# Branch splits between the head norms, another bank pair for the first late gate, and an out projection with a loop of its own

## The reference: two layers of a hybrid decoder trunk

```python
h = h + 0.5 * swiglu(rmsnorm(h, norm_ffn1), ...)              # D_FF = 2816
x = rmsnorm(h, norm_mix)
z = x @ w_in + b_in                                           # mixers' inputs and 4 x 1024 gate columns
# four branches, 256 wide each
br_conv = silu(layernorm(conv + conv_b, conv_ln_g, conv_ln_b))
br_ret  = silu(r_g) * head_norm(r_o, ret_gn, center=True)
br_gla  = silu(g_r) * head_norm(g_o, gla_gn, center=False)
br_diff = head_norm(d_o, diff_subln, center=False) * (1.0 - lam_init)
gate   = sigmoid(gates.reshape(B, L, 4, 1024))
merged = einsum('blnc,ncd,blnd->bld', branches, w_branch, gate)
h = h + merged @ w_out
h = h + 0.5 * swiglu(rmsnorm(h, norm_ffn2), ...)
```

## Time and profile before

| | |
|---|---|
| median of 3 runs | 3060.79 us (3059.02 to 3063.26) |
| the profiled execution | 3066.44 us, of which the span of the core is 3064.9 |
| TensorE's mean granted clock | 0.975 of full speed |
| busy: PE, VectorE, ScalarE, GpSimd | 95%, 68%, 42%, 4% of the span |
| HBM | 104 GB/s over the span |

### The profile page before, as it was taken

One profiled execution on the slowest core, in us unless ns is written; L12 is line 12 of the kernel. 1 busy time (PEld: TensorE's weight loads), 2 busy tenths in 40 slices (PEclk: granted clock), 3 DMA queues, 4 the chain that ended last, 5 costly groups with the idle time before them and its releaser, 6 DMA issues.

```text
span 3064.9 us, 60838 instructions
## 1 busy us (share of the span) xinstructions
PE 2908.1 (95%) x21640; PEld 2779.2 (91%) x21640; DVE 2088.7 (68%) x3658; ACT 1285.0 (42%) x2206; POOL 120.8 (4%) x219
## 2 busy tenths in 40 slices
PE   4999999999899999999989999999989999999998
PEld 3999999887778989999989999998877889999998
DVE  7999534567556669996489993346664566799955
ACT  5555323335215245554255552233441242555533
POOL 0000001220000000000000000112100000000000
PEclk9999999999889999999999999999998999999999
DMA  3222225552213312223212222437422243122222
GB/s 112 96 87 98 97 82 176 164 191 81 82 59 142 136 59 88 85 93 110 83 57 96 95 98 96 139 117 202 143 79 80 74 148 119 56 96 94 97 97 88
DMA packets 102125, 320.89 MB, mean 105 GB/s; under 512 B 13503, under 2 KB 30063, under 8 KB 100272
## 3 DMA queue, kind: packets, MB, share of 16 engines
q1 hardware_dynamic: 89424, 277.03, 26.2%
q0 software_dynamic: 12512, 41.43, 4.3%
HBM read 290.62 MB, written 29.12 MB: 104 GB/s over the span
## 4 chain that ended last, share of the span: by engine, by line
PE 82%; DVE 6%; issue 6%; ACT 3%; POOLq 1%; DMA 1%; POOL 1%; DVEq 0%; ACTq 0%
PE ps L1226 41%; PE ps L1255 32%; PE ps L1386 3%; PE ps L1640 1%; PE ps L1238 1%; PE ps L1502 1%; POOLq L562 1%; DVE w_lo L1746 1%; DMA rets_out<-ss 0%; ACT hT L1013 0%; PE ps L1518 0%; POOL vpage L563 0%; PE ps L1480 0%; ACT w_hi L714 0%; DVE x_more L1832 0%
## 5 line engine op out<-in xcount | busy, mean ns | idle before, releaser
L1746 DVE TENSOR_TENSOR w_lo<-w_raw,w_hi 128x1024 fp32r<-128x1024 f32 x240 | 292.8, 1223 | 399.5 <-ACT w_hi L674 394.2
L1255 PE MATMUL ps<-x_more,w_hi 128*128 128x296 f32 x2112 | 462.1, 300 | 14.6 <-DVE p_copy L1902 12.6
L674 ACT ACTIVATE w_hi<-w_raw 128x1024 fp32r<-128x1024 f32 x224 | 235.5, 1054 | 528.4 <-PE ps L1226 198.2
L1255 PE MATMUL ps<-x_hi,w_hi 128*128 128x296 f32 x1408 | 426.3, 303 | 25.1 <-ACT p_copy L778 11.8
L1255 PE MATMUL ps<-x_hi,w_lo 128*128 128x296 f32 x1408 | 425.6, 302 | 0.0
L1255 PE MATMUL ps<-x_lo,w_hi 128*128 128x296 f32 x1408 | 425.3, 302 | 0.0
L714 ACT ACTIVATE w_hi<-w_raw 128x512 fp32r<-128x512 f32 x445 | 272.3, 629 | 306.8 <-PE ps L1255 192.7
L1226 PE MATMUL ps<-x_hi,w_hi 128*128 128x296 f32 x1600 | 377.7, 318 | 14.7 <-ACT hT L1013 9.3
L1255 PEld LDWEIGHTS ps<-x_more,w_hi 128*128 128x128 f32 x2112 | 353.7, 190 | 16.0 <-issue 13.6
L1226 PE MATMUL ps<-x_hi,w_lo 128*128 128x296 f32 x1600 | 356.5, 305 | 0.0
L1226 PE MATMUL ps<-x_lo,w_hi 128*128 128x296 f32 x1600 | 356.2, 305 | 0.0
(11 more groups left out here) (350 smaller groups left out, 4986.9 us busy)
## 6 DMA issues: line engine op xcount, KB each, us to landing
w_raw<-wstream SPq DMA_DIRECT2D x420, 512.0 KB, 3.5
kpage<-cache_k SPq DMA_DIRECT2D x128, 128.0 KB, 3.0
vpage<-cache_v POOLq DMA_DIRECT2D x128, 128.0 KB, 3.3
gate_rows<-hT SPq DMA_DIRECT2D x48, 296.0 KB, 2.1
d_sg<-gate_rows SPq DMA_DIRECT2D x16, 888.0 KB, 4.6
h_rows<-hT SPq DMA_DIRECT2D x2, 1480.0 KB, 6.1
hT<-h_rows SPq DMA_DIRECT2D x2, 1480.0 KB, 10.6
hT<-h_in SPq DMA_DIRECT2D x4, 592.0 KB, 8.3
```

What stands on the lines that cost most here:

```text
L674: act.activation(w_hi[:, slot, :, :], w_raw[:, slot, :, :], ACT.Copy).then_inc(weights_high, 1)
L1255: mm = pe.matmul(ps[:, bank, 0:HALF], wp[:, k, :], xp, start=new and k == 0 and n == 0, stop=k == KH - 1 and n == 2, skip_group_check=True)
L1746: v.tensor_tensor(w_lo[:, slot, :, :], w_raw[:, slot, :, :], w_hi[:, slot, :, :].bitcast(F32), ALU.subtract).then_inc(weights_low, 1)
```

## The change

1. *Head norms and branches on VectorE.* After norms 0 to 3 VectorE multiplies tiles 4 and 5 by their SiLU gates, waits for the mixers' stores, makes `br_hi` of the first four tiles of `FINISHED` itself (`tensor_copy`) and then their `br_lo`. Norms 4 to 6, the convolution's bias and tiles 2 and 3 follow. The low parts of weights 22 and 23, which stood between these steps, stand at the end of `branches`.
2. *ScalarE.* `br_hi` is made for the last four tiles only. Gates 22 and 23 are taken out of PSUM without their weight splits; the tanh of the convolution stands ahead of gate 23; the splits of weights 22 and 23 stand behind the tanh of late gate 0.
3. *The late gate of m = 0* is in pair 2, and PE doesn't wait for the tanh of gate 23 before it. Before branch 2 of m = 0 (also pair 2) PE waits for that late gate's tanh.
4. *The order in a merge step.* `m_hi` and `m_lo` are made before the second weight split of the step, no longer after it. The loops over m of PE and ScalarE are unrolled.
5. *Out projection.* PE has a function of its own for it, unrolled. It opens when branch 1 of m = 7 is taken (pair 1 empty) and seven tiles are ready. There is no drain, and the wait for all four branches stands behind unit 0.
6. *SP.* The first two `load_gates` are issued right after the weight load of f = 21, no longer after all stores of gate rows.

```diff
@@ -443,6 +443,11 @@
+def late_pair(m):
+return 3 if m else 2
 FINISHED = (6, 7, 4, 5, 2, 3, 0, 1)
@@ -530,12 +535,13 @@
         load_at(U_GATES + 2 * RING + f)
+        if f == 21:
+            sp.wait_ge(gla_s_state, 1)
+            load_gates(0)
+            load_gates(1)
     for s in range(STAGES):
         sp.wait_ge(gates_stored[s], 16 * KD * EARLY // STAGES)
     sp.wait_ge(h_spilled, 16)
-    sp.wait_ge(gla_s_state, 1)
-    load_gates(0)
-    load_gates(1)
     sp.dma_start(hT[:, 0:SPILLED, :], h_rows).then_inc(h_back, 16)
@@ -1141,37 +1147,39 @@
         square(4 + i, branch_tiles[tile])
-    gate_out(l, 22)
+    gate_activated(l, 22)
     for i in range(4, 7):
         act.wait_ge(hn_normed, i - 3)
         root(i)
     for i in range(4, 7):
         inverse(i)
-    gate_out(l, 23)
-def branches():
+def branches(l):
+    act.wait_ge(hn_normed, 7)
+    act.wait_ge(conv_done, 2)
+    for i in range(2):
+        act.activation(hn_root[:, i, :], Z[:, CG + i, :], ACT.Tanh, scale=0.5).then_inc(act_tanh, 1)
+    gate_activated(l, 23)
     act.wait_ge(mixers_stored, 16 * MIXER_STORES)
     for n, b in enumerate(FINISHED):
-        if n == 4:
-            act.wait_ge(conv_done, 2)
-            for i in range(2):
-                act.activation(hn_root[:, i, :], Z[:, CG + i, :], ACT.Tanh, scale=0.5).then_inc(act_tanh, 1)
-        act.wait_ge(hn_normed, 7)
-        act.wait_ge(br_ready, n + 1)
-        act.activation(br_hi[:, b, :], branch_tiles[b], ACT.Copy).then_inc(br_high, 1)
+        if n >= 4:
+            act.wait_ge(br_ready, n + 1)
+            act.activation(br_hi[:, b, :], branch_tiles[b], ACT.Copy).then_inc(br_high, 1)
 def gates(l):
-    with act.Fori(0, 2) as i:
-        for mm in range(4):
-            m = i * 4 + mm
-            quad, slot = l * QUADS + U_MERGE // RING + i * 2 + mm // 2, mm % 2 * 2
-            unit_done(quad, slot)
-            act.activation(split_cols(d_late[:, :]), pair(3), ACT.Tanh, scale=0.5, bias=hb[:, ds(m + 8 * EARLY, 1)]).then_inc(gate_tanh, 1)
-            split_high(quad + 1, slot)
-            act.wait_ge(merged_steps, m * 3 + 3)
-            split_high(quad + 1, slot + 1)
-            act.activation(m_hi[:, ds(m, 1), :], d_acc[:, 0:1, :], ACT.Copy, scale=0.5).then_inc(merged_high, 1)
+    for m in range(KD):
+        quad, slot = l * QUADS + U_MERGE // RING + m // 2, m % 2 * 2
+        unit_done(quad, slot)
+        act.activation(split_cols(d_late[:, :]), pair(late_pair(m)), ACT.Tanh, scale=0.5,
+                       bias=hb[:, m + 8 * EARLY:m + 8 * EARLY + 1]).then_inc(gate_tanh, 1)
+        if m == 0:
+            for f in (22, 23):
+                split_high(l * QUADS + (U_GATES + f) // RING + 1, f % RING)
+        split_high(quad + 1, slot)
+        act.wait_ge(merged_steps, m * 3 + 3)
+        act.activation(m_hi[:, m, :], d_acc[:, 0, :], ACT.Copy, scale=0.5).then_inc(merged_high, 1)
+        split_high(quad + 1, slot + 1)
     act.drain().then_inc(mixers_left, 1)
@@ -1205,7 +1213,7 @@
     head_norms(l)
-    branches()
+    branches(l)
     gates(l)
...
@@ -1328,18 +1336,12 @@
...
@@ -1698,22 +1700,38 @@
     pe.sem_inc(phases_entered, 1)
-    with pe.Fori(0, 2) as i:
-        for mm in range(4):
-            m = i * 4 + mm
-            quad, slot = l * QUADS + U_MERGE // RING + i * 2 + mm // 2, mm % 2 * 2
-            unit_ready(quad, slot)
+    for m in range(KD):
+        quad, slot = l * QUADS + U_MERGE // RING + m // 2, m % 2 * 2
+        unit_ready(quad, slot)
+        if m:
             pe.wait_ge(gate_tanh, m + KD * EARLY)
-            products(3, slot, (0, 8), 0, x_hi, x_lo).then_inc(units_multiplied, 1)
-            unit_ready(quad, slot + 1)
-            pe.wait_ge(br_split, 8)
-            for b in range(4):
-                if b in (0, 3):
-                    pe.wait_ge(branch_taken, m * 4 + 4 + b // 3)
-                last = products(BRANCH_BANKS[b], slot + 1, (2 * b, 2 * b + 2), 2 * b, br_hi, br_lo)
-                last.then_inc(*((branch_products, 1) if b < 3 else (units_multiplied, 1)))
-    pe.wait_ge(branch_taken, 4 * KD + 4)
-    pe.drain().then_inc(mixers_left, 1)
+        products(late_pair(m), slot, (0, 8), 0, x_hi, x_lo).then_inc(units_multiplied, 1)
+        unit_ready(quad, slot + 1)
+        pe.wait_ge(br_split, 8)
+        for b in range(4):
+            if b in (0, 3):
+                pe.wait_ge(branch_taken, m * 4 + 4 + b // 3)
+            if m == 0 and b == 2:
+                pe.wait_ge(gate_tanh, KD * EARLY + 1)
+            last = products(BRANCH_BANKS[b], slot + 1, (2 * b, 2 * b + 2), 2 * b, br_hi, br_lo)
+            last.then_inc(*((branch_products, 1) if b < 3 else (units_multiplied, 1)))
+def out_projection(l):
+    for m in range(KD):
+        pe.wait_ge(residual_added, l * 24 + 8 + m + 1)
+        unit_ready(l * QUADS + (U_OUT + m) // RING, m % RING)
+        bank = OUT_PAIRS[m % 4]
+        if m == 0:
+            pe.wait_ge(branch_taken, 4 * KD + 2)
+            pe.wait_ge(merged_ready, l * KD + KD - 1)
+            products(bank, 0, (0, KD - 1), 0, m_hi, m_lo, stop=False)
+            pe.wait_ge(merged_ready, l * KD + KD)
+            products(bank, 0, (KD - 1, KD), KD - 1, m_hi, m_lo, start=False).then_inc(units_multiplied, 1)
+            pe.wait_ge(branch_taken, 4 * KD + 4)
+            pe.sem_inc(mixers_left, 1)
+        else:
+            products(bank, m % RING, (0, KD), 0, m_hi, m_lo).then_inc(units_multiplied, 1)
@@ -1733,7 +1751,7 @@
     gates(l)
-    residual(l, 8, U_OUT, (8,), m_hi, m_lo)
+    out_projection(l)
     ffn(l, 1, U_FFN2)
@@ -2405,38 +2423,49 @@
-    for i in range(7):
-        if i == 4:
-            gate_low(l, 22)
+    def finished(b, c):
+        v.scalar_tensor_tensor(branch_tiles[b], Z[:, c, :], 0.5, branch_tiles[b], ALU.mult, ALU.mult).then_inc(br_ready, 1)
+    for i in range(4):
+        normed(i)
+    v.sem_inc(br_ready, 2)
+    v.wait_ge(hn_normed, 4)
+    finished(4, GR)
+    finished(5, GR + 1)
+    v.wait_ge(mixers_stored, 16 * MIXER_STORES)
+    for n in range(4):
+        b = FINISHED[n]
+        v.wait_ge(br_ready, n + 1)
+        v.tensor_copy(br_hi[:, b, :], branch_tiles[b]).then_inc(br_high, 1)
+    for n in range(4):
+        branch_low(n)
+    for i in range(4, 7):
         normed(i)
     v.wait_ge(hn_normed, 7)
     for j in range(2):
         ins = v.tensor_scalar(Z[:, CG + j, :], Z[:, CG + j, :], prm[:, P_LB + j:P_LB + j + 1], None, ALU.add)
     ins.then_inc(conv_done, 1)
-    v.sem_inc(br_ready, 2)
-    for b, c in ((4, GR), (5, GR + 1), (2, RG), (3, RG + 1)):
-        v.scalar_tensor_tensor(branch_tiles[b], Z[:, c, :], 0.5, branch_tiles[b], ALU.mult, ALU.mult).then_inc(br_ready, 1)
+    finished(2, RG)
+    finished(3, RG + 1)
+def branch_low(n):
+    b = FINISHED[n]
+    v.wait_ge(br_high, n + 1)
+    v.tensor_tensor(br_lo[:, b, :], branch_tiles[b], br_hi[:, b, :].bitcast(F32), ALU.subtract).then_inc(br_split, 1)
 def branches(l):
-    def low(n):
-        b = FINISHED[n]
-        v.wait_ge(br_high, n + 1)
-        v.tensor_tensor(br_lo[:, b, :], branch_tiles[b], br_hi[:, b, :].bitcast(F32), ALU.subtract).then_inc(br_split, 1)
-    v.wait_ge(br_ready, 6)
-    for n in range(4):
-        low(n)
-    gate_low(l, 23)
     for n in range(2):
         v.wait_ge(act_tanh, 5 + n)
         link(v.tensor_scalar(hn_root[:, n, :], hn_root[:, n, :], 1.0, 0.5, ALU.add, ALU.mult))
         v.tensor_tensor(branch_tiles[n], branch_tiles[n], hn_root[:, n, :], ALU.mult).then_inc(br_ready, 1)
     v.wait_ge(br_ready, 8)
     for n in range(4, 8):
-        low(n)
+        branch_low(n)
+    gate_low(l, 22)
+    gate_low(l, 23)
 def gates(l):
-    v.wait_ge(mixers_stored, 16 * MIXER_STORES)
     clear_sum(3 * l + 3)
@@ -2458,11 +2487,11 @@
                     v.tensor_tensor(d_acc[:, 0, :], d_acc[:, 0, :], d_acc[:, 1, :], ALU.add).then_inc(merged_steps, 1)
-            split_low(quad + 1, slot + 1)
             v.wait_ge(merged_steps, m * 3 + 3)
             v.wait_ge(merged_high, m + 1)
             v.scalar_tensor_tensor(m_lo[:, ds(m, 1), :], d_acc[:, 0:1, :], 0.5, m_hi[:, ds(m, 1), :].bitcast(F32),
                                    ALU.mult, ALU.subtract).then_inc(merged_ready, 1)
+            split_low(quad + 1, slot + 1)
             v.wait_ge(merged_ready, l * KD + m + 1)
```

More of the change, by code:

```diff
@@ L1320, in ffn, with residual @@
                 pe.sem_inc(units_multiplied, 2 * KF)
-            def residual(l, r0, first, blocks, xh, xl, hidden=None):
+            def residual(l, r0, first, blocks, xh, xl, hidden):
                 units = len(blocks)
@@ L1330, in residual @@
                             bank = OUT_PAIRS[j]
-                            if hidden is not None and j == 0:
+                            if j == 0:
                                 for k in range(blocks[u]):
@@ L1336, in residual @@
                                 last.then_inc(units_multiplied, 1)
-                            elif hidden is None and j == 0:
```

(4 more changed lines are left out.)

## The result

Five runs of either kernel gave 3044.38 us (3040.80 to 3045.83) after and 3060.06 us (3057.14 to 3063.26) before: a ratio of **0.9946, 95% interval 0.9931 to 0.9960**, 12 to 21 us less. Ratios in this document are the ones on record; they aren't the quotients of the two medians beside them, from which they differ by up to 0.0017. The forecast was 3043.0 us. The profiled execution of the changed kernel took 3044.62 us, its span 3043.1.

What follows compares the result with a forecast made beforehand. PE, busy 95% of 3064.9 us, bounds the kernel through waits and slow clock. Gains 6.1 + 5.6 + 7.6 = 19.3 us, one dip leaves 17.8: 3048.6 profiled, median 5.65 lower, 3043.0 us; 8 in 10 for 3037 to 3051.

Steps and rivals of the forecast that it cites:

- The late gate: Opening of the merge, m = 0: starts at 966.50 instead of 967.50, without the 0.84 us wait for gate 23's tanh.
- VectorE's queue: Opening of the merge: copies and subtractions hidden before norm 4; first branch product at 973.8, after 0.6 us of PE idling.
- The new stall: Before branch 3 of m = 0, PE waits 1.8 us in each layer until VectorE has taken branch 0.
- The queues: SP's loads: earlier gate loads and later weight loads cost nothing; weights issued 13 us before need, landing in 3.5 us.
- The out projection: After m = 7: 3.8 us a layer, 2.2 wait and restart plus 1.6 clock; 7.6 us in both layers.
- The sum: Both layers' merges: 6.1 + 5.6 + 7.6 = 19.3 us gained, if the new stall costs only its length.
- The dip: PE's clock falling behind the new stall, 1.5 us each; one taken for two layers, leaving a gain of 17.8 us.
- The time: Whole kernel: profiled execution 3048.6 us, median 5.65 us below it, so 3043.0 us, 0.58% less.
- (b): Rival: PE's slow clock lasts after the new stall in both layers, 5 to 6 us each; 3050 to 3052 us; chance 0.10.
- (c): Rival: half delivers; branch chain not shortened, or out projection finds another wait; 3050 to 3054 us; chance 0.10.
- (d): Rival: stall only moves; branch 3's wait grows and out projection waits for m_lo; 3058 to 3061 us; chance 0.05.
- (e): Rival: slower, SP's queue holds a load and weights of m = 3 arrive late; 3067 us or more; chance 0.03.

Runs made afterwards that it cites:

- e2_bank_only: Kernel before with PE's and ScalarE's loops over m unrolled and the late gate of m = 0 on pair 2, without its wait for gate 23; ratio 1.0011.
- e9_same_bank: Changed kernel with the late gate of m = 0 back on bank pair 3, behind gate 23's tanh; 3056.46 us, ratio 0.9963.
- e5_late_gate_loads: Changed kernel with SP's first two gate loads back behind all stores of gate rows; 3056.73 us, ratio 0.9986.
- the two experiments: Kernel before with the new out projection and earlier m_hi and m_lo, ratio 0.9985; changed kernel with the old out projection, ratio 0.9954.
- e4_old_out: Changed kernel with the old out projection (wait for four branches, drain), the new order of m_hi and m_lo kept; 3050.71 us, ratio 0.9954.
- e10_scalar_and_first: Changed kernel with VectorE's memset before weight split 22, branch 0 right behind it, and the first four br_hi on ScalarE; 3046.94 us, ratio 0.9943.
- e8_longer_stall: Changed kernel with two more waited memsets on VectorE at m = 0, ahead of the existing one; one execution, 3050.92 us.
- e6_scalar_splits: Changed kernel with the first four high parts of the branches made by ScalarE, no copies on VectorE; 3043.96 us, ratio 0.9933.

## Why the prediction was right, step by step

- **The late gate.** Right: no wait there, and it starts 1.0 us earlier, as put. `e2_bank_only` shows that this is worth nothing while the last `br_lo` comes late. The 8 us of `e9_same_bank` are another thing, which the sum didn't price: with the old pair PE waits 2.49 us for gate 23's tanh, which the change itself lets end 1.6 us later than before, and loses clock behind it.
- **VectorE's queue.** The copy took 0.46 us, its lower bound. The first branch product was put at 973.8 on the scale of before, 35.97 us after the first square; it came at 35.87. VectorE's first taking was put at 979.6, 41.77 after; it came at 41.74. The low parts ended 7.1 us after the start of the late gate, inside the 7.3 that the prediction gave as its limit.
- **The new stall.** It is there, in both layers, where it was put. Forecast 1.8 us, measured 1.54: PE went on 0.05 us after VectorE's operation had ended, where I had charged 0.24, the lag seen before the first branch product. The small rest is that PE fell idle 0.15 us later than put.
- **The queues.** In layer one SP issued the moved weight loads at 975.1 and 976.3 and no wait for a `w_lo` followed in m = 1 to 3. The prediction called the earlier gate loads harmless and gave them no value. It didn't ask what they would have cost in their old place. Of the parts that it read too lightly this is the largest, 16.5 us by the merges when undone (`e5_late_gate_loads`); the bank pair is the other.
- **The out projection.** 7.6 us forecast; 7.2 and 7.3 by the two experiments. The prediction let the earlier `m_lo` count for "no wait"; by the estimate above there would have been none with the old order either.
- **The sum.** 19.3 us without a dip of the clock, 19.7 measured by the two merges. Up to the late tanh of m = 1 the layers gain 6.4 and 5.9 us (6.1 and 5.6 forecast), behind it 7.4 together (7.6 forecast), so the mechanism and each of its terms hold within half a microsecond.
- **The dip.** The step from 19.3 to 17.8 took one dip for the two layers. In the profiles that have this stall at its 1.54 us (the changed kernel twice and `e4_old_out`) it comes six times, and there was no dip, though a 0.48 us gap stood shortly ahead of it each time. The forecast's basis, that the gap's length decides, is not what the later runs show (below), and the profile of before already spoke against it. The earlier trace rows is a 1.59 us gap in layer one that left the clock at 1.00. The same gap in layer two of the same profile had the lower level behind it (0.63):

```profile
2372.99 0.50 PE L1640 MATMUL ps<-Z 32*128 32x128 f32 x8 [1.59 <-DVE g_sc L2330]
```

```profile
2372.99:2376.99 4.00, 4.00 (x28) 3.34 (x28) 1.48 (x2) 0.00 (x0) 0.00 (x0) 0.63 0.18 71
```

- **The time.** By the medians the gain is 15.7 and 16.4 us in two comparisons, by the ratios 16.5 and 20.2, with intervals that hold 17.8 as well as 19.7. Whether the runs that were not profiled had dips there is open. That the median came within 1.4 us of the forecast is in part luck: the profiled execution was forecast at 3048.6 and took 3044.62, and the 5.65 us by which a median was to lie below its profile were 0.24.
- **The rivals.** (b) isn't seen: in the changed kernel and its variants the clock never stayed down for more than some 4 us behind a merge stall. (c) and (d) didn't come: both halves delivered. (e) didn't come; SP's slack was enough. Nor was the time lost again at the second feed-forward: PE's wait for `p_copy` there is 5.5 us in both profiles.

## What to carry to other kernels

When several edits shorten one chain, undo each from the finished kernel and also try it alone: the bank pair was worth 0 alone and 8 us together with the new order of ScalarE's tanh, the copies on VectorE 0 in company of a stall and 1.6 us a layer without it. A step moved off one path is queued ahead of something else: write out the queue behind it and you have the next stall, and often its cure, a new order on the same engine. And a load that is early enough today may be what the edit rests on once everything behind it moves; ask what each line of a diff would cost if it were left out.

## What the runs showed of the hardware

The level of TensorE's clock behind a gap isn't told by the gap's length. 2.08 us of idling at the same point of the same code (`e10_scalar_and_first`) lowered it in one layer and not in the other, and 3.02 us in `e8_longer_stall` did the same; 2.09 us left it at 1.00 in both layers of `e6_scalar_splits` and so did 2.25 us in `e9_same_bank`, while 1.87 us before the old out projection lowered it in both. Behind the 1.54 us stall it stayed up six times of six, behind the 1.59 us gap of the earlier trace rows it stayed up in one layer of before and fell in the other. In the merge, gaps of 4.9 us and more lowered it each time. What decides between the two outcomes for a shorter gap these runs don't show. Where it fell behind a gap of 1.9 to 3 us the price was 1.5 to 1.6 us, beside the gap itself. A sum for a single gap of 1.5 to 3 us should carry both values. A VectorE copy from fp32 to fp32r of 128x592 in SBUF takes 0.46 us, against 0.77 for the subtraction of the same size.
